# Low parts of a drain moved between VectorE and GpSimd, and the down-projections' waits moved to where each weight piece is used

## The chip, the cores and the metric

The kernel runs on one core of a Trainium2 chip. The time is device microseconds of one launch. The kernel before takes 1396.87 us (median of 3 runs, 1396.63 to 1397.98).

## The reference, cut to what matters

Two layers of a diffusion transformer over 256 tokens `x` and 256 context tokens `ctx`, width 1024. Layer zero mixes with a gated linear attention (hgrn2, 8 heads, forward and backward), layer one with a Mamba-2 mixer; each is followed by a convolutional feed-forward block of width 2816.

```python
for l in range(DEPTH):                                  # 2
    mx = split(silu(c) @ ada_w[l] + ada_b[l], 6)        # shifts, scales and gates
    hx = modulate(rmsnorm(x, pre_norm[l, 0]), mx[0], mx[1])
    yx = mixer(hx, hc)                                  # l = 0: hgrn2, l = 1: mamba2
    x = x + mx[2] * rmsnorm(yx, post_norm[l, 0])
    hx = modulate(rmsnorm(x, pre_norm[l, 1]), mx[3], mx[4])
    x = x + mx[5] * rmsnorm((silu(conv(hx @ w_up_a)) * (hx @ w_up_v)) @ w_down, post_norm[l, 1])
# hgrn2, per head and direction: f = lb + (1 - lb) * sigmoid(fz); k = 1 - f
# att = tril((q * exp(cumsum log f)) @ (k * exp(-cumsum log f)).T), plus the state carried between chunks
# y = (rmsnorm(o) * norm_w * silu(g)) @ hg_w_out
```

In layer zero the same is done for `ctx`, so its stages have 512 columns (`T`), those of layer one after the mixer 256 (`SEQ`).

## The kernel before, in words

All products of weights run as three matmuls of split numbers: a tile's high part times a weight's high part, its low part times the high part, and its high part times the weight's low part (`gemm`, L2095 to L2097). A weight arrives in pieces of 128 x 1024 (`subs`, 4 slots of `wraw`). For each piece SP loads it (`load`, L609), ScalarE writes the high part `wh` (`split_hi`, L799), VectorE or GpSimd writes the low part `wl` = `wraw` - `wh` (`split_lo`, L1312; `part`, L700), and TensorE waits for the count of low parts (`need_sub`). Activations are split likewise: ScalarE writes `hh` (`y_high`, L984), and the low part `hl` = `yT` - `hh` is written by VectorE's `y_low` (L1562) or GpSimd's (L745).

Each engine's order is written out by hand; semaphores are counted. Stage one is the hgrn2 mixer: for each of 8 heads, VectorE's `gate_products(h, d)` works in two halves, forward (d = 0) and backward (d = 1). A half clamps ScalarE's exponential (L1591, `e_clamped`), lets ScalarE take logarithm, exponential and logarithm again (L940 to L944), scans (L1607 or L1609), lets ScalarE take three exponentials (L949 to L953, `en_ready`), and forms the products (L1644 to L1657), with `qk_ready` after L1656 and `qin_ready` after L1657.

The drain is the end of this stage, the last head (7), whose own attention has no next head's projections to lie beside. TensorE's order there is: `att(7, 0)`, `ke(7, 0)`, the first k-tiles of the output projection's tiles 0 to 2 (`hg_early((0, 1), range(3))`, L2299 to L2301; it needs pieces 40 to 42 and the low parts 0 and 1 of `yT`), `kv(7, 0)` (L2237; it waits for ScalarE's `ke_rows`, L978), an ada block (L2161), `o_turn(6)` (L2268), `att(7, 1)` (L2210), `ke(7, 1)` (L2228; its bank must be emptied by `states(7, 0)`, L1536 and L1540), and then further k-tiles. Pieces 40 to 47 are the eight column tiles of the output projection.

GpSimd does nothing between the constants and this drain; then it waits for all of `qin_ready` and writes the low parts 2 to 6. VectorE writes 0, 1 and 7. `split_lo(42)` stands in `gate_products(7, 0)` between the small sums (L1633) and the wait on `en_ready`; `split_lo(43)`, `mask_att(7, 0)` and `states(7, 0)` stand after `gate_products(7, 1)`.

Each feed-forward block works in two halves of 12 and 10 k-tiles. A column tile of the down-projection takes two pieces, the first with 8 k-tiles, the second with the other 4 or 2, and TensorE waits for both before the tile's first matmul. Inside a tile, `need(k)` waits for GpSimd's low parts of the activations (`fl_ready`, L720) at the first and the last k-tiles. In the first half the eight tiles run in a loop, in the second they are written out. VectorE splits the pieces of the first down tile between the taps of the last convolution tile, and the next two behind it.

## Time and profile before

| | |
|---|---|
| median of 3 runs | 1396.87 us |
| the profiled execution | 1396.92 us |
| its span | 1395.2 us |
| TensorE (PE) busy | 1327.7 us, 95% of the span |
| VectorE (DVE) busy | 901.8 us, 65% |
| ScalarE (ACT) busy | 646.6 us, 46% |
| GpSimd (POOL) busy | 304.5 us, 22% |

The busy share is an average over stages with different limits; what a change is worth is read from the stage in which it lies. Times of a row are us from the start of the span. PE is a matmul, PEld a weight load that overlaps it, SPq the queue of the engine that issues DMAs.

### The profile page before, as it was taken

The page shows a single profiled execution, that of the slowest core. Times are in us where ns is not written, and L with a number is a line of the kernel's source. Part 1 is how long each engine was busy: PE and PEld are TensorE (multiplying, and loading weights), DVE is VectorE, ACT ScalarE, POOL GpSimd, SP SyncE. Part 2 cuts the span into 40 slices and gives each one's busy share as a digit, 9 for nine tenths or more (in the row PEclk, how much of TensorE's full clock was granted, in tenths as well). Part 3 has the DMA queues.
Part 4 walks back from the last instruction along what each step waited for, and adds up shares of the span by engine and source line. Part 5 has one row for each costly group of instructions (what it writes and reads, how often), then busy time and mean ns, then how long its engine had stood idle before and what let it go on. Part 6 is the DMA issues. An engine that isn't in the chain of part 4 may idle for free.

```text
span 1395.2 us, 21261 instructions
## 1 busy us (share of the span) xinstructions
PE 1327.7 (95%) x7893; PEld 1116.3 (80%) x7893; DVE 901.8 (65%) x1730; ACT 646.6 (46%) x1020; POOL 304.5 (22%) x203
## 2 busy tenths in 40 slices
PE   5999999999998999999999989999999988899997
PEld 3678888888665788888888757888888877899997
DVE  5567777677588644322456778777777957765573
ACT  4435444444355533223333256555555645554554
POOL 1000000000200654105551000211111300680961
PEclk9999999999999999999999999999999999999999
DMA  9543343335461632334324424433333465455743
GB/s 346 178 133 124 121 132 126 122 96 177 151 210 32 181 94 72 90 105 121 91 68 136 121 91 121 151 91 91 92 93 98 128 216 147 120 167 170 207 136 107
DMA packets 274787, 183.16 MB, mean 131 GB/s; under 512 B 6642, under 2 KB 249106, under 8 KB 274706
## 3 DMA queue, kind: packets, MB, share of 16 engines
q1 hardware_dynamic: 274162, 180.00, 42.7%
q10 hardware_dynamic: 544, 2.10, 0.4%
q8 instruction: 49, 0.80, 0.2%
q14 instruction: 32, 0.26, 0.1%
HBM read 181.03 MB, written 1.05 MB: 131 GB/s over the span
## 4 chain that ended last, share of the span: by engine, by line
PE 77%; DVE 12%; ACT 6%; issue 2%; DMA 1%; SPq 1%; POOL 0%; DVEq 0%; ACTq 0%
PE bank L2095 20%; PE bank L2097 20%; PE bank L2096 20%; DVE wl L1312 2%; PE bank L2161 2%; ACT tmp L845 1%; DMA gates<-in_ada_w 1%; ACT wh L799 1%; DVE hl L1408 1%; DVE tmp L1430 1%; PE bank L2210 1%; DVE conv L1760 1%; PE bank L2237 1%; PE bank L2665 1%; ACT hh L849 1%
## 5 line engine op out<-in xcount | busy, mean ns | idle before, releaser
L2095 PE MATMUL bank<-hh,wh 128*128 128x512 f32 (+1 forms) x1298 | 460.2, 355 | 11.1 <-DVE wl L1312 5.5
L2097 PE MATMUL bank<-hh,wl 128*128 128x512 f32 (+1 forms) x1298 | 455.5, 351 | 0.0
L2096 PE MATMUL bank<-hl,wh 128*128 128x512 f32 (+1 forms) x1298 | 455.2, 351 | 0.0
L799 ACT ACTIVATE wh<-wraw 128x1024 fp32r<-128x1024 f32 (+2 forms) x265 | 256.4, 985 | 99.6 <-PE bank L2097 97.3
L1312 DVE TENSOR_TENSOR wl<-wraw,wh 128x1024 fp32r<-128x1024 f32 (+2 forms) x187 | 206.0, 1124 | 121.7 <-ACT wh L799 121.6
L2095 PEld LDWEIGHTS bank<-hh,wh 128*128 128x128 f32 x1298 | 246.8, 190 | 45.9 <-DVE wl L1312 7.8
L2097 PEld LDWEIGHTS bank<-hh,wl 128*128 128x128 f32 x1298 | 246.7, 190 | 32.4
L2096 PEld LDWEIGHTS bank<-hl,wh 128*128 128x128 f32 x1298 | 247.0, 190 | 30.3
L1760 DVE SCALAR_TENSOR_TENSOR conv<-bank,pv,conv 128x189 f32<-128x189 f32 (+3 forms) x396 | 173.3, 438 | 131.7 <-ACT conv L1064 103.6
L700 POOL TENSOR_TENSOR wl<-wraw,wh 128x1024 fp32r<-128x1024 f32 x78 | 186.9, 2406 | 316.6 <-ACT wh L799 316.0
L2095 PE MATMUL bank<-fh,wh 128*128 128x512 f32 (+1 forms) x352 | 120.0, 341 | 3.5 <-DVE wl L1312 3.1
L2096 PE MATMUL bank<-fl,wh 128*128 128x512 f32 (+1 forms) x352 | 119.0, 338 | 0.0
L2097 PE MATMUL bank<-fh,wl 128*128 128x512 f32 (+1 forms) x352 | 119.0, 338 | 0.0
L745 POOL TENSOR_TENSOR hl<-yT,hh 128x512 fp32r<-128x512 f32 x13 | 18.5, 1448 | 371.6 <-DVE gates L1657 357.9
L2095 PEld LDWEIGHTS bank<-fh,wh 128*128 128x128 f32 x352 | 66.2, 188 | 12.1 <-issue 1.7
L2097 PEld LDWEIGHTS bank<-fh,wl 128*128 128x128 f32 x352 | 66.2, 188 | 8.0
L2096 PEld LDWEIGHTS bank<-fl,wh 128*128 128x128 f32 x352 | 66.3, 188 | 7.9
L777 POOL TENSOR_TENSOR wx<-xtok,wtk 128x512 f32<-128x512 f32 x16 | 16.9, 1055 | 246.0 <-ACT xtok L1197 162.1
L2110 PE MATMUL bank<-hh,wh 128*128 128x512 f32 (+2 forms) x119 | 48.7, 409 | 15.2 <-DVE hl L1408 14.0
L1064 ACT ACTIVATE conv<-bank,pv 128x512 f32<-128x512 f32 (+1 forms) x44 | 29.4, 668 | 72.8 <-PE bank L2097 72.8
L720 POOL TENSOR_TENSOR fl<-prod,fh 128x512 f32 (+3 forms) x44 | 49.9, 1134 | 55.1 <-ACT fh L1080 55.1
L2110 PEld LDWEIGHTS bank<-hh,wh 128*128 128x128 f32 (+1 forms) x119 | 24.2, 203 | 30.3 <-issue 11.9
(337 smaller groups left out, 1918.9 us busy)
## 6 DMA issues: line engine op xcount, KB each, us to landing
wraw<-in_ffn_w_up SPq DMA_DIRECT2D x88, 512.0 KB, 3.9
araw<-in_ada_w SPq DMA_DIRECT2D x40, 1024.0 KB, 7.0
wraw<-in_mb_w_in SPq DMA_DIRECT2D x48, 512.0 KB, 4.0
wraw<-in_hg_w_in SPq DMA_DIRECT2D x40, 512.0 KB, 3.8
wraw<-in_ffn_w_down SPq DMA_DIRECT2D x32, 512.0 KB, 3.9
wraw<-in_mb_w_out SPq DMA_DIRECT2D x16, 512.0 KB, 4.6
gates<-in_ada_w SPq DMA_DIRECT2D x5, 1024.0 KB, 9.3
wraw<-in_hg_w_out SPq DMA_DIRECT2D x8, 512.0 KB, 4.8
```

Source lines behind the costliest of these rows:

```text
L700: pool.tensor_tensor(wl[:, n % SLOTS, 0:size], wraw[:, n % SLOTS, 0:size], wh[:, n % SLOTS, 0:size].bitcast(F32), ALU.subtract).then_inc(w ...
L720: pool.tensor_tensor(fl[:, bass.ds(i * 2 + c, 1), 0:w], prod[:, c % 2, 0:w].unsqueeze(1), fh[:, bass.ds(i * 2 + c, 1), 0:w].bitcast(F32), ...
L745: pool.tensor_tensor(hl[:, k, :], yT[:, k, :], hh[:, k, :].bitcast(F32), ALU.subtract).then_inc(yl_ready, 1)
L799: act.activation(wh[:, n % SLOTS, 0:size], wraw[:, n % SLOTS, 0:size], ACT.Copy).then_inc(w_hi, 1)
L1064: act.activation(conv[:, u, 0:n], bank[2 * u if src is None else src][:, 0:n], ACT.Identity, scale=pv[:, bass.ds(i * 2 + (cw + c), 1)], bi ...
L1312: ins = dve.tensor_tensor(wl[:, s, lo:hi], wraw[:, s, lo:hi], wh[:, s, lo:hi].bitcast(F32), ALU.subtract)
L1760: ins = V.scalar_tensor_tensor(out=o(conv[:, u, :]), in0=src(bank[up]), scalar=pv[:, bass.ds(i * 2 + (cw + row * FT + c), 1)], in1=o(conv[ ...
L2095: pe.matmul(dst, W, hi(k), start=(k == 0), stop=False, **skip)
L2096: pe.matmul(dst, W, lo(k), start=False, stop=False, **skip)
L2097: ins = pe.matmul(dst, L, hi(k), start=False, stop=(k == nk - 1), **skip)
L2110: pe.matmul(dst, W, hi(k), start=(k == 0), stop=False, skip_group_check=True)
L2161: ins = pe.matmul(bank[plan.bank(key)][32 * j:32 * j + 32, :], scc[:, 4 * half + j, :], ada_chunk(n, half, j), start=(half == 0), stop=(ha ...
```

## The change

In the drain, the low parts 0 and 1 of `yT` go from VectorE to GpSimd, ahead of GpSimd's wait on `qin_ready`; `mask_att(7, 0)` takes the place of `y_low(1)` inside `gate_products(7, 1)`; and `split_lo(42)` goes from before the wait on `en_ready` to behind the last product of `gate_products(7, 0)`. In the down-projections, TensorE waits for a tile's first piece before the tile and for the second at the k-tile that first uses it; the last tile of layer zero keeps both waits ahead of it.

```diff
@@ gpsimd
+        y_low(0, range(2))
         pool.wait_ge(qin_ready, 2 * HEADS)
         y_low(0, range(2, KT - 1))
@@ vector, gate_products(h, d)
             if end:
                 head_mean(HEADS - 2)
-                y_low(0)
             dve.wait_ge(sig_ready, n + 1)
...
             if h < HEADS - 1:
                 split_lo(5 * h + 6 + d)
-            elif d == 0:
-                split_lo(5 * h + 7)
-            else:
+            elif d == 1:
                 head_norm(HEADS - 2)
-                y_low(1)
+                mask_att(h, 0)
             dve.wait_ge(en_ready, n + 1)
...
             V.tensor_tensor(ch(Dd), ch(C), s[:, 1, :].unsqueeze(2).to_broadcast([P, NCH, CH]), ALU.mult).then_inc(qin_ready, 1)
+            if h == HEADS - 1 and d == 0:
+                split_lo(5 * h + 7)
@@ vector, after the heads
         split_lo(at["y", 0, 3])
-        mask_att(HEADS - 1, 0)
         states(HEADS - 1, 0)
@@ tensor, down-projection, first half
                         for u in range(2):
-                            for j in range(2):
-                                by, count = lo_of[d0 + 2 * u + j]
-                                pe.wait_ge(w_lo[by], i * 4 + count)
+                            by, count = lo_of[d0 + 2 * u]
+                            pe.wait_ge(w_lo[by], i * 4 + count)
                             pe.wait_ge(plan.freed["act"], i * 2 + (reads["act"] + u - 1))
-                            gemm(bank[4 + u][:, 0:n], tile_w(d0 + 2 * u), fhi, flo, nf, need=need).then_inc(psum_ready, 1)
+
+                            def need_both(k, u=u):
+                                if k == KT:
+                                    by, count = lo_of[d0 + 2 * u + 1]
+                                    pe.wait_ge(w_lo[by], i * 4 + count)
+                                need(k)
+
+                            gemm(bank[4 + u][:, 0:n], tile_w(d0 + 2 * u), fhi, flo, nf, need=need_both).then_inc(psum_ready, 1)
@@ tensor, down-projection, second half
                         need_sub(d0 + 2 * m)
-                        need_sub(d0 + 2 * m + 1)
...
                         if l == 0 and m == KT - 1:
+                            need_sub(d0 + 2 * m + 1)
                             last_tile(1, 0, 1, n, key, tile_w(d0 + 2 * m), fhi, flo, nf)
...
                         plan.wait_free(pe, key)
-                        plan.done(gemm(bank[plan.bank(key)][:, 0:n], tile_w(d0 + 2 * m), fhi, flo, nf, need=need), key)
+
+                        def need_last(k, m=m):
+                            if k == KT:
+                                need_sub(d0 + 2 * m + 1)
+                            need(k)
+
+                        plan.done(gemm(bank[plan.bank(key)][:, 0:n], tile_w(d0 + 2 * m), fhi, flo, nf, need=need_last), key)
```

## Rows read from the trace of the kernel before

**Rows 1.** Page, part 4: shares of the chain that ended last, by engine.
```profile
PE 77%; DVE 12%; ACT 6%; issue 2%; DMA 1%; SPq 1%; POOL 0%; DVEq 0%; ACTq 0%
```

**Rows 2.** TensorE's waits: line, releaser, us in total, times, longest.
```profile
PE bank L2299 <- DVE hl L1562: 2.4, 1, 2.4
```

**Rows 3.** Chain of waits, 340 to 430 us: start, us, what.
```profile
358.70 0.79 PE bank L2299
...
362.49 0.67 PE bank L2237 x6
...
365.01 0.59 PE bank L2268 x4
...
367.47 0.59 PE bank L2228 x4
```

**Rows 4.** Timeline of VectorE, drain: start, us, instructions, idle before and its releaser.
```profile
346.97 1.22 DVE L1312 TENSOR_TENSOR wl<-wraw,wh 128x1024 fp32r<-128x1024 f32 x1
348.10 0.68 DVE L1644 TENSOR_TENSOR gates<-tmp,gates 128x512 f32<-128x512 f32 x1
...
351.38 0.69 DVE L1657 TENSOR_TENSOR gates<-gates,sm 128x512 f32<-128x512 f32 x1
351.98 0.42 DVE L1591 TENSOR_SCALAR gates<-gates 128x512 f32<-128x512 f32 x1
...
353.76 0.55 DVE L1604 TENSOR_SCALAR gates<-gates,omlb 128x512 f32<-128x512 f32 x1 [0.17 <-ACT gates L942]
...
361.23 0.68 DVE L1656 TENSOR_TENSOR gates<-gates,sm 128x512 f32<-128x512 f32 x1
...
364.52 0.73 DVE L1540 SCALAR_TENSOR_TENSOR st<-st,sm,bank 128x128 f32<-128x128 f32 x2
```

**Rows 5.** Timeline of ScalarE, drain.
```profile
347.45 0.25 ACT L953 ACTIVATE sm<-sm 128x80 f32<-128x80 f32 x1
...
350.21 1.15 ACT L984 ACTIVATE hh<-yT 128x512 fp32r<-128x512 f32 x2
...
358.47 0.59 ACT L978 ACTIVATE ket<-bank 128x512 f32<-128x512 f32 x1
```

**Rows 6.** Instructions of line L745: duration in ns, least, median, most.
```profile
L745 POOL TENSOR_TENSOR hl<-yT,hh x13: 1262/1292/2193, 362.6 to 1127.4; 128x512 fp32r<-128x512 f32 x13
```

**Rows 7.** Timelines of VectorE and GpSimd, 1250 to 1290 us, where they meet.
```profile
1261.66 2.36 DVE L1312 TENSOR_TENSOR wl<-wraw,wh 128x1024 fp32r<-128x1024 f32 x2
1265.85 1.83 DVE L1312 TENSOR_TENSOR wl<-wraw,wh 128x1024 fp32r<-128x1024 f32 x2 [1.83 <-ACT wh L799]
...
1262.27 1.20 POOL L720 TENSOR_TENSOR fl<-prod,fh 128x256 fp32r<-128x256 f32 x1 [3.59 <-ACT fh L1080]
```

**Rows 8.** Timelines of GpSimd and VectorE, 1104 to 1108 us.
```profile
1104.48 8.71 POOL L745 TENSOR_TENSOR hl<-yT,hh 128x512 fp32r<-128x512 f32 x6
...
1106.22 1.51 DVE L2018 TENSOR_TENSOR h<-hs,bc 128x256 f32<-128x256 f32 x1
```

**Rows 9.** Stretches: us, busy PE, PEld, DVE, ACT, POOL (instructions), granted clock, DMA.
```profile
358.50:360.00 1.50, 1.30 (x3) 1.11 (x4) 1.47 (x4) 1.50 (x5) 0.00 (x0) 0.50 0.24 57
...
415.76:418.37 2.61, 0.00 (x0) 0.03 (x1) 2.61 (x7) 0.75 (x3) 0.00 (x0) 1.00 0.61 170
418.37:422.00 3.63, 3.63 (x9) 1.71 (x10) 2.58 (x5) 2.15 (x4) 0.00 (x0) 1.00 0.43 129
```

**Rows 10.** Timelines of TensorE and VectorE: start of `hg_early`, entries of layer one's down-projections.
```profile
354.00 0.48 PE L2299 MATMUL bank<-hh,wh 128*128 128x512 f32 x1
...
1256.89 1.21 DVE L1312 TENSOR_TENSOR wl<-wraw,wh 128x1024 fp32r<-128x1024 f32 x1
...
1257.74 0.60 PE L2173 MATMUL bank<-ident,asum 128*128 128x128 f32 x4
1259.86 0.36 PE L2095 MATMUL bank<-fh,wh 128*128 128x256 f32 x1 [1.52 <-DVE wl L1312]
...
1263.84 0.28 PE L2095 MATMUL bank<-fh,wh 128*128 128x256 f32 x1
...
1353.47 0.36 PE L2095 MATMUL bank<-fh,wh 128*128 128x256 f32 x1 [1.55 <-DVE wl L1312]
...
1357.28 0.39 PE L2095 MATMUL bank<-fh,wh 128*128 128x256 f32 x1 [0.38 <-POOL fl L720]
```

## The prediction

> **What bounds the kernel now.** I read the shares of the chain that ended last first: TensorE holds 77% of it, VectorE 12%, ScalarE 6% [rows 1]. So the time changes only where TensorE stands still, or where another engine carries the chain. TensorE's list of waits gives the places that the diff can touch. The plainest is one wait of 2.4 us for VectorE's `hl` of L1562 (`y_low`) [rows 2]. The chain of waits places it in the drain of stage one: at 358.70, and from there on TensorE's own work follows without a break [rows 3]. VectorE's timeline shows what stands ahead of it: `split_lo(42)` at 346.97, products up to L1657 at 351.38, the clamp L1591 of the next half at 351.98, then that half's products up to L1656 at 361.23 [rows 4]. Behind the wait the granted clock was 0.50 [rows 9].
>
> **The drain, VectorE's side.** (1) `split_lo(42)` leaves its place before the wait on `en_ready`. The product behind it, L1644, started at 348.10, but ScalarE's L953, for which it waits, ends at 347.45 + 0.25 = 347.70 [rows 4, 5]. L1644 can start at 347.74, so 0.36 us is gained; the rest of the 1.22 filled a wait. `qk_ready` of the first half comes 0.36 earlier, L1657 would start at 351.02 and make room at 351.62 (351.98 - 0.36).
> (2) The split now stands there, ahead of the clamp L1591, and takes 1.14 (348.10 - 346.97 by rows 4). ScalarE's three steps of the second half wait for that clamp, and VectorE's products for them. Clamp: 351.62 + 1.14 = 352.76 instead of 351.98, +0.78. Alone, the move makes the second half later. SP gains a late step too: the load that takes piece 42's slot waits for the split. Its own piece is used after 390 us, and what SP queues behind it waits for TensorE's next ada block anyway, so that costs nothing.
> (3) `y_low(0)` leaves VectorE in front of L1604, where VectorE waited for ScalarE with 0.17 us to spare [rows 4]: worth nothing. `y_low(1)` (0.60 to the next start) becomes `mask_att(7,0)` (0.63): +0.03. After the last product `states(7,0)` comes behind `split_lo(43)` alone, 0.63 sooner in the order.
> (4) The two low parts on GpSimd. ScalarE's two copies start at 350.21 and take 1.15 together [rows 5], the first is done by about 350.84, so GpSimd asks from 350.9, amid VectorE's L1656, L1657 and the moved split. A free L745 takes 1.26 to 1.29 us, the longest took 2.19 [rows 6]. What the engines do to each other shows where they met. At 1261.66 VectorE's two splits took 2.36, the same pair 1.83 at 1265.85, and GpSimd's `fl` took 1.20. Taken whole and in turns: first split to 1262.73, `fl` 0.74 to 1263.47, second split 0.55 to 1264.02, which is what the rows say to 0.01 [rows 7]. From 1104.48 six L745 took 8.71 us, and a VectorE product of 256 columns (L2018) took 1.51, twice what L1644 needs for 512 [rows 4, 8]. So a GpSimd instruction and a VectorE one with two inputs in SBUF exclude each other, and turns alternate even when the next of VectorE's is queued.
> By that: `y_low(0)` gets its turn at 351.03 and ends at 352.3; L1657 ends at 352.9; `y_low(1)` runs to 354.1; the moved split to 355.2; the clamp starts at 355.1, +3.1 us. If GpSimd gets no turn between L1656 and L1657, the clamp is at +2.1 (no further turn taken ahead of the clamp) to +3.3. The low end of (2) and (4) together is +0.8, with no hindrance at all. I take +3.1, by the nearest rows, two queued splits.
>
> The Trainium skill says more than the rows do (SBUF — State Buffer, section "SBUF: two separate sides"): GpSimd and VectorE share a pair of ports under an exclusive lock held for the whole instruction, against every VectorE instruction with two SBUF inputs. By that L1657 is hit as the splits are; were only splits hit, the clamp would come some 0.7 us sooner and the sum be that much smaller. The rule speaks against this half of the change, and rows 7 agree.
>
> **The drain, TensorE's side.** `att(7,0)` starts 0.36 earlier, so `hg_early` is reached at 353.65, before 354.00 [rows 10]. It needs pieces 40 to 42, and 42 is done at 355.2: TensorE idles 1.6 us in place of 2.37. Its 18 matmuls of 0.23 end at 359.5 (before: 362.49). Next late is `kv(7,0)`, which waits for ScalarE's L978; that stands behind the second half's exponents and ended at 358.47 + 0.59 = 359.06 [rows 5], 3.1 later is 362.2: a new idle of 2.7 us. `kv`, the ada block and the turn take 365.60 - 362.49 = 3.11 [rows 3], so `att(7,1)` starts at 365.3; its own `qk_ready`, 361.91 + 3.1 = 365.0, is just inside [rows 4]. `ke(7,1)` is 1.88 behind, at 367.2. But it wants the bank that `states(7,0)` empties: VectorE's products end at 365.6, the split of 43 takes 1.1, `states` 1.05: 367.8, against 367.47 before, +0.3 us. If the clock falls in the idle of 2.7 us, as it did in that of 2.37 (0.50 from 358.50 to 360.00), the 3.11 us of work lose about 1.4, and `ke(7,1)` starts at 368.6, +1.1. A gap of 2.61 us at 415.76 kept 1.00, so it need not fall [rows 9]. I take +1.1. GpSimd's `y_low(2)` ends at 368.0, in time; (3) to (6), 1.45 each by rows 8, end at 374, before TensorE asks. From there TensorE is without a wait to the end of the stage, and what follows hangs on it, so the shift stays.
>
> **The down-projections.** At the two entries of layer one TensorE stood still for a short second piece, 1.52 us to 1259.86 and 1.55 to 1353.47 [rows 10]. First: the first piece is split at 1256.89 + 1.21 = 1258.10, the ada turn ends at 1258.34, so the tile starts 1.5 us sooner. Its last k-step, though, also waits (`fl_ready`) for GpSimd's last `fl`, 1262.27 + 1.20 = 1263.47 [rows 7]. The k-steps are 0.356 apart, so the twelfth stood at 1263.84 and is wanted at 1262.3; it will start at 1263.52, and a restart costs 0.11. The second tile stood 0.06 for its own short piece, which is now waited for later. 0.3 us is left of 1.52. Second: there the tenth k-step already waited for `fl`, until 1357.28 [rows 10], and VectorE's, ScalarE's and GpSimd's way to it is untouched. Nothing is left of 1.55. TensorE's waits show none of this kind in layer zero: nothing. The moved wait stands once in each tile at a k-step between matmuls; three k-steps of each tile carry a wait for `fl` now, and where it is met long before the starts stay 0.12 apart. I take 0; bounds -0.1 and +0.3 us over all tiles. Behind it only the same tile's rest is queued.
>
> **Sum.** +1.1 - 0.3 = +0.8 us. The profiled execution took 1396.92 us (span 1395.2 and 1.7 around it), 0.05 over the median of the runs. Forecast: 1397.7 us. A measurement of this kernel tells about 0.2%, 2.8 us, from no change; the forecast is no change.
>
> **Rivals.**
> A. The engines don't hold each other up here. For it: L745 and the gate products have not met in this trace. Against: rows 7 and 8. The clamp is then 0.78 late only; TensorE runs to 357.9, waits for ScalarE to 359.9, `att(7,1)` is at 363.0, `ke(7,1)` at 365.5 by `states`, 1.95 earlier. With the 0.3 of the down-projections: 1394.7 us. 20%.
> B. The slower one: TensorE's clock at the next gap. At 415.76 it stood 2.61 us and kept 1.00, where the shorter one of 2.37 lost it [rows 2, 9]. So whether a gap of this length costs the clock depends on where it falls, and any shift of the drain moves it. Behind it stand the matmuls of the sums, 3.63 us busy on the chain [rows 9]; half speed through most of them costs about 1.9. It decides as soon as that stretch reads 0.50: 1397.7 + 1.9 = 1399.6 us. 22%.
> C. VectorE keeps its turn through the queued products, clamp at +2.1: `kv` at 361.2 after 1.7 us of idle with the clock kept, `ke(7,1)` at 366.8, -0.7. With the 0.3: 1395.9 us. 15%.
> D. The down-projections gain their full 3.07 us. For it: both idles are put down to `wl`. Against: `fl` is 0.4 us behind in the first and already waited for in the second. 1394.9 us. 3%.
>
> **How the numbers follow.** Forecast 40%, A 20, B 22, C 15, D 3. A and D lie 2 us below the median and pass 0.2% in about half of their cases, the clock at later gaps adding or taking up to 1.7: faster 0.15. B lies 2.7 above and passes it in half, and a tail of the forecast with it: slower 0.16. Same 0.69. The range reaches from just under A to just over B: 1394.3 to 1399.9.
>
> **What would show it.** Right: L745 twice near 351; L1657 or the moved L1312 longer than 0.69 and 1.22; the clamp near 355; TensorE's wait on L1562 gone, and in its place one of L2299 on L1312 and one of L2237 on L978; the first down tile of layer one from 1258 with an idle before its last k-step for L720. Wrong: a clamp before 353.5 (A), `ke(7,1)` before 366 us, a clock of 1.00 from `kv(7,0)` on, or an entry in layer one that gains over 1 us.

## The result, and the profile after

| | before | after |
|---|---|---|
| median of the runs (22 each) | 1396.92 us (1393.06 to 1398.86) | 1400.01 us (1397.21 to 1401.32) |
| the profiled execution | 1396.92 us, span 1395.2 | 1398.98 us, span 1397.2 |
| TensorE busy | 1327.7 us | 1327.1 us |
| VectorE busy | 901.8 us | 903.3 us |
| GpSimd busy | 304.5 us | 308.4 us |

The ratio after to before is 1.0016 [1.001, 1.0022]: 2.2 us slower (1.4 to 3.1), where 0.8 was forecast. It lies inside what was called no change, though the upper end of the interval passes the 2.8 us that were named for that, and its sign is certain. The medians of the table lie further apart, 3.1 us, because the times of the kernel after form two groups and the median falls into the upper one (the means lie 2.4 apart); the text goes by the ratio. By the ratio the kernel takes 1399.1 us, inside the range of 1394.3 to 1399.9; its median alone stands 0.1 us above it.

In the kernel after, line numbers are shifted by one or two: the split is L1313, the clamp L1592, the last two products L1654 and L1655, ScalarE's `ket` L979, `hg_early` L2298, `kv` L2236, `ke` L2227.

First comes VectorE's timeline in the drain of the kernel after (start, us, instructions, idle before and its releaser). It answers to [rows 4].

```profile
346.57 0.69 DVE L1642 TENSOR_TENSOR gates<-tmp,gates 128x512 f32<-128x512 f32 x1 [0.69 <-ACT sm L954]
...
349.25 0.68 DVE L1654 TENSOR_TENSOR gates<-gates,sm 128x512 f32<-128x512 f32 x1
349.85 1.76 DVE L1655 TENSOR_TENSOR gates<-gates,sm 128x512 f32<-128x512 f32 x1
351.54 2.28 DVE L1313 TENSOR_TENSOR wl<-wraw,wh 128x1024 fp32r<-128x1024 f32 x1
353.74 0.41 DVE L1592 TENSOR_SCALAR gates<-gates 128x512 f32<-128x512 f32 x1
355.52 0.55 DVE L1604 TENSOR_SCALAR gates<-gates,omlb 128x512 f32<-128x512 f32 x1 [0.77 <-ACT gates L943]
...
365.65 0.73 DVE L1541 SCALAR_TENSOR_TENSOR st<-st,sm,bank 128x128 f32<-128x128 f32 x2
```

Then GpSimd and ScalarE there, which answer to [rows 5, 6].

```profile
349.76 2.98 POOL L745 TENSOR_TENSOR hl<-yT,hh 128x512 fp32r<-128x512 f32 x2 [345.07 <-ACT hh L985]
```

```profile
346.29 0.25 ACT L954 ACTIVATE sm<-sm 128x80 f32<-128x80 f32 x1
...
360.24 0.58 ACT L979 ACTIVATE ket<-bank 128x512 f32<-128x512 f32 x1
```

The reader is to see the two engines take turns. GpSimd's two low parts run from 349.76 to 352.74. In that time the product L1655 takes 1.76 us instead of 0.69, and the moved split L1313 2.28 instead of 1.22: each is 1.07 and 1.06 us longer, the time for which it waited on one of GpSimd's low parts. The clamp behind them comes at 353.74.

TensorE's timeline in the drain of the kernel after, which answers to [rows 3], and then its granted clock by stretches, which answers to [rows 9] (us, busy PE, PEld, DVE, ACT, POOL, clock, DMA).

```profile
353.88 0.50 PE L2298 MATMUL bank<-hh,wh 128*128 128x512 f32 x1 [1.16 <-DVE wl L1313]
...
360.88 1.65 PE L2236 MATMUL bank<-vtok,ket 128*128 128x128 f32 x6 [2.62 <-ACT ket L979]
362.45 2.68 PE L2160 MATMUL bank<-araw,scc 128*32 128x512 f32 x16
...
367.53 0.66 PE L2227 MATMUL bank<-ident,gates 128*128 128x128 f32 x4
```

```profile
360.88:362.40 1.52, 1.52 (x6) 1.35 (x6) 1.49 (x5) 1.52 (x4) 0.00 (x0) 0.50 0.00 0
362.40:365.60 3.20, 3.20 (x22) 1.05 (x22) 3.20 (x7) 0.88 (x2) 1.24 (x1) 0.74 0.07 7
416.00:418.53 2.53, 0.00 (x0) 0.03 (x1) 2.53 (x6) 0.67 (x3) 0.00 (x0) 1.00 0.61 181
418.53:422.16 3.63, 3.63 (x5) 1.55 (x6) 2.57 (x5) 0.58 (x1) 0.00 (x0) 0.53 0.45 133
```

The sums and the entry of layer zero's up-projections, TensorE's timelines: first the kernel before, then the kernel after.

```profile
418.37 1.10 PE L2405 MATMUL bank<-sq,ones 128*128 128x512 f32 x2 [2.61 <-DVE sq L1381]
...
430.45 0.77 PE L2110 MATMUL bank<-hh,wh 128*128 128x512 f32 x1 [3.98 <-DVE hl L1408]
```

```profile
418.53 1.93 PE L2404 MATMUL bank<-sq,ones 128*128 128x512 f32 x2 [2.60 <-DVE sq L1382]
...
432.31 0.76 PE L2109 MATMUL bank<-hh,wh 128*128 128x512 f32 x1 [3.98 <-DVE hl L1409]
```

The wait for `hl` of L1562 [rows 2] is gone, and two stand in its place: 1.16 us for piece 42 and 2.62 us for `ket`. Behind the second the clock is 0.50. And behind the idle ahead of the sums at 418.53, 2.60 us long where it had been 2.61, the clock is 0.53 where it had been 1.00. From the first sum to the up-projections it is 13.78 us instead of 12.08.

The entries of layer one's down-projections, from TensorE's timeline of the kernel after; they answer to [rows 10].

```profile
1260.20 0.60 PE L2172 MATMUL bank<-ident,asum 128*128 128x128 f32 x4
...
1265.97 0.39 PE L2094 MATMUL bank<-fh,wh 128*128 128x256 f32 x1 [1.02 <-POOL fl L720]
...
1354.25 0.39 PE L2094 MATMUL bank<-fh,wh 128*128 128x256 f32 x1 [0.26 <-DVE wl L1313]
...
1359.34 0.39 PE L2094 MATMUL bank<-fh,wh 128*128 128x256 f32 x1 [1.63 <-POOL fl L720]
```

From the ada turn to the last k-step of the first tile it is 5.77 us instead of 6.10: 0.33 gained. Laid side by side, the two profiled executions give the whole account (start of the same instruction, us):

| | before | after | difference | what came since the line above |
|---|---|---|---|---|
| ScalarE's small exponential, forward half ("the mark") | 347.45 | 346.29 | -1.16 | +0.38 up to 89 us, then -1.54 by the clock behind an idle of 2.4 us there: 0.50 before, 1.00 after |
| `ke(7,1)` | 367.40 | 367.53 | +0.13 | the drain: +1.29 |
| first sum behind the output projection | 418.37 | 418.53 | +0.16 | |
| first up-projection, layer zero | 430.45 | 432.31 | +1.86 | the clock at the sums: +1.70 |
| first up-projection, layer one | 1178.76 | 1181.23 | +2.47 | the clock behind an idle of 2.93 us near 1129, 0.50 in both but for longer after: +0.61 |
| last k-step, first down tile | 1263.84 | 1265.97 | +2.13 | the down-projections: -0.33 |
| tenth k-step, ninth down tile | 1357.28 | 1359.34 | +2.06 | -0.07 |
| end of the span | 1395.2 | 1397.2 | +2.0 | |

The terms ahead of the mark and the one near 1129 lie where the change touches nothing. So one pair of executions does not price the change: its own terms are +1.29 in the drain, -0.4 in the down-projections, and perhaps the +1.70. The experiments had to settle whether the last belongs to it.

### The profile page after: what moved, and what is told of

It reads as the page before. It is cut to its first block, busy times and chain, and to the rows that moved or that the text cites. A ratio compares the mean times of both kernels' runs of the same rounds, so it can differ in the third digit from the quotient of the medians.

```text
span 1397.2 us, 21265 instructions
## 1 busy us (share of the span) xinstructions
PE 1327.1 (95%) x7893; PEld 1116.0 (80%) x7893; DVE 903.3 (65%) x1728; ACT 646.6 (46%) x1020; POOL 308.4 (22%) x205
## 4 chain that ended last, share of the span: by engine, by line
PE 77%; DVE 13%; ACT 7%; issue 2%; DMA 1%; POOL 0%; DVEq 0%; ACTq 0%
PE bank L2094 20%; PE bank L2096 20%; PE bank L2095 20%; DVE wl L1313 3%; PE bank L2160 2%; ACT tmp L846 1%; ACT wh L800 1%; DVE conv L1759 1%; DVE hl L1409 1%; DVE tmp L1431 1%; PE bank L2209 1%; PE bank L2236 1%; PE bank L2676 1%; ACT hh L850 1%; PE bank L2663 1%
## 5 line engine op out<-in xcount | busy, mean ns | idle before, releaser
L1313 DVE TENSOR_TENSOR wl<-wraw,wh 128x1024 fp32r<-128x1024 f32 (+2 forms) x187 | 207.0, 1129 | 121.6 <-ACT wh L800 121.5
L745 POOL TENSOR_TENSOR hl<-yT,hh 128x512 fp32r<-128x512 f32 x15 | 22.4, 1520 | 369.0 <-ACT hh L985 357.4
L720 POOL TENSOR_TENSOR fl<-prod,fh 128x512 f32 (+3 forms) x44 | 50.2, 1141 | 55.0 <-ACT fh L1081 55.0
```

Of the source, the lines that this page charges most:

```text
L720: pool.tensor_tensor(fl[:, bass.ds(i * 2 + c, 1), 0:w], prod[:, c % 2, 0:w].unsqueeze(1), fh[:, bass.ds(i * 2 + c, 1), 0:w].bitcast(F32), ...
L745: pool.tensor_tensor(hl[:, k, :], yT[:, k, :], hh[:, k, :].bitcast(F32), ALU.subtract).then_inc(yl_ready, 1)
L1313: ins = dve.tensor_tensor(wl[:, s, lo:hi], wraw[:, s, lo:hi], wh[:, s, lo:hi].bitcast(F32), ALU.subtract)
```

## The experiments

Positions are given in us behind the mark (the start of ScalarE's small exponential of the forward half), so that what happened earlier drops out. Before: clamp 4.53, `ket` 11.02, `kv(7,0)` 14.88, `ke(7,1)` 19.95 by the timeline (the chain of waits [rows 3] has this start 0.07 later). After: clamp 7.45, `ket` 13.95, `kv(7,0)` 14.59, `ke(7,1)` 21.24. Ratios are to runs of the kernel before on the same chip.

**One part alone.**

`down_only`: the kernel before with the down-projections' waits moved. Part of the edit is shown; the second wait goes to the k-tile that first uses the piece, as in the change.

```diff
-                            for j in range(2):
-                                by, count = lo_of[d0 + 2 * u + j]
-                                pe.wait_ge(w_lo[by], i * 4 + count)
+                            by, count = lo_of[d0 + 2 * u]
+                            pe.wait_ge(w_lo[by], i * 4 + count)
...
-                        need_sub(d0 + 2 * m + 1)
...
```

> Only the waits of the down-projections are changed, the drain is the one of before. My theory (the wait for fl takes the place of the wait for the short piece): the first down tile of layer one, first half, starts about 1.5 us sooner after the last up tile, then TensorE idles about 1.0 us before its last k-step for GpSimd's L720, and the eight tiles end 0.2 to 0.4 us sooner than before; second half: tile starts 1.2 us sooner and waits 1.6 us for L720 instead of 0.4, nothing is gained. Sum -0.3 us. Rival D (both idles are real gains): -3.1 us. Rival (waits inside a tile cost issue time): slower by 0.3 us or more. Times of single runs spread by some us from one to the next, so the verdict is read from the two entries.

Measured 1396.15 us (10 runs) against 1397.20, ratio 0.9997 [0.9987, 1.0006]. TensorE's timeline of this kernel at the same k-step:

```profile
1257.25 0.60 PE L2173 MATMUL bank<-ident,asum 128*128 128x128 f32 x4
...
1263.03 0.39 PE L2095 MATMUL bank<-fh,wh 128*128 128x256 f32 x1 [1.03 <-POOL fl L720]
```

5.78 us instead of 6.10, and the second entry's wait for `fl` grew from 0.38 to 1.64. The 1.52 and 1.55 us that stood on `wl` were worth 0.3 and less than 0.1, as the theory had it.

`split_only`: the kernel before with `split_lo(42)` behind the last product.

```diff
-            elif d == 0:
-                split_lo(5 * h + 7)
...
+            if h == HEADS - 1 and d == 0:
+                split_lo(5 * h + 7)
```

> Only split_lo(42) is moved behind the last product of the first half; both low parts stay on VectorE. Measured in the trace from the start of ScalarE's small exponential of the first half (L953, 347.45 before) to ke(7,1) (L2228, 367.47 before): 20.02 us before. My theory (the split filled a wait and now stands ahead of the clamp): clamp 4.53 + 0.78 = 5.3 us after that mark, and ke(7,1) at 20.8 us, +0.8. Rival (the split's 1.1 us come off the chain as a move to a place where it does not matter): 18.9 to 20.0 us.

Measured 1398.42 us (10 runs) against 1397.20, ratio 1.0005 [0.9995, 1.0014]. The clamp is at 5.31, 0.78 later than before, to the hundredth what steps (1) and (2) said. The split took 1.22 there: without GpSimd beside it, it is not long. `ke(7,1)` is at 20.21, +0.26 where +0.8 was expected, but the two profiles differ in the clock: this one kept 1.00 in the drain behind an idle of 2.69 us, the kernel before lost it behind 2.37. Against `before_clk` below, which keeps the clock too and has `ke(7,1)` at 19.43, it is +0.78, the full delay of the clamp.

`pool_only`: the kernel before with the two low parts on GpSimd; split and mask stay.

```diff
+        y_low(0, range(2))
         pool.wait_ge(qin_ready, 2 * HEADS)
...
-                y_low(0)
...
-                y_low(1)
```

> Only the two low parts go to GpSimd; split_lo(42) and mask_att(7,0) stay where they were. Mark as in split_only (20.02 us before to ke(7,1); clamp at 4.53 us). My theory (whole instructions in turns): GpSimd's first low part gets its turn behind L1656, L1657 takes 1.9 us in place of 0.69, and the clamp comes at 5.8 us if a tensor_scalar with one input is not hit, at 7.1 us if it is. ke(7,1) then at 18.6 us (bound by states) or at 19.8 to 20.6. Rival A (no hindrance): clamp at 4.5, L1657 0.69 us, ke(7,1) at 17.5 to 18.2.

Measured 1401.01 us (8 runs) against 1397.20, ratio 1.0024 [1.0014, 1.0035]. VectorE's timeline of this kernel, then TensorE's:

```profile
351.27 1.76 DVE L1656 TENSOR_TENSOR gates<-gates,sm 128x512 f32<-128x512 f32 x1
352.95 1.49 DVE L1592 TENSOR_SCALAR gates<-gates 128x512 f32<-128x512 f32 x1
```

```profile
361.16 0.94 PE L2236 MATMUL bank<-vtok,ket 128*128 128x128 f32 x6 [2.89 <-ACT ket L979]
...
366.07 0.86 PE L2267 MATMUL bank<-ident,tmp 128*128 128x128 f32 x4 [2.12 <-DVE attm L1552]
366.73 1.91 PE L2209 MATMUL bank<-gates 128*128 128x128 f32 x8
```

This is the dearest of the three parts. With no split queued, GpSimd's second turn falls on the clamp itself: 1.49 us instead of 0.42. It has only one input in SBUF, so the prediction had counted it as free of this, while the expectation of this run had left it open. And `o_turn(6)` waits 2.12 us for `mask_att(7,0)`, which still stands behind the second half's products. `ke(7,1)` is at 22.66, +2.71 and 2 us later than the latest that was expected. What lies beyond the expectation is mostly the clock: it was kept behind the idle of 2.89 us and lost behind the 2.12 us of this second wait (0.50 from 366.73 to 369.70; the eight matmuls of L2209 take 1.91 us instead of 1.06). From `o_turn(6)` to `ke(7,1)` it is 3.94 us, where `after_nomask` and `before_clk`, with the clock at 1.00 there, take 2.43 and 2.44: some 1.5 of the 2.71 us are the clock's.

`after_nomask` asks what the moved mask is worth: the kernel after with `mask_att(7,0)` put back behind `split_lo(43)`.

```diff
-                mask_att(h, 0)
...
+        mask_att(HEADS - 1, 0)
         states(HEADS - 1, 0)
```

> The changed kernel, but mask_att(7,0) stays behind split_lo(43) as before. Seen in pool_only: o_turn(6), which takes the bank that mask_att empties, waited 2.1 us for it. Theory (that move carries part of the change): o_turn waits about 2 us, ke(7,1) at 23 us or later after the mark in place of 21.2. Rival (mask_att's place is free either way): 21.2 us.

Measured, in one run, 1400.90 us. `o_turn(6)` waits 0.48 us for the mask and `ke(7,1)` is at 21.93: 0.69 later than in the kernel after, less than the theory had, because the lost clock ahead of it already makes `o_turn` late, and behind it no clock is lost as it was in `pool_only`. So the mask's new place takes back part of what the low parts cost.

**GpSimd kept off VectorE's queue.**

`gated`: the low parts go to GpSimd, but only once the last product of the forward half of head 7 is done; the split stays in its old place; mask and down-projections as in the change. GpSimd's part of the edit, against the kernel before:

```diff
+        pool.wait_ge(qin_ready, 2 * HEADS - 1)
+        y_low(0, range(2))
         pool.wait_ge(qin_ready, 2 * HEADS)
```

> The change, but split_lo(42) stays where it was and GpSimd waits for the last product of the first half (15 counts of qin_ready) before low parts 0 and 1, so that these lie beside VectorE's clamp, sum and waits for ScalarE. My theory: L1657 keeps 0.69 us, the clamp stays at 4.5 us after the mark, L1604 or the scan is delayed by 0 to 0.6 us by the second low part, TensorE runs hg_early without a wait and then idles about 1.4 us for ScalarE's L978 with its clock kept; ke(7,1) at 17.8 us after the mark (bound by states) in place of 20.0. With the down-projections' 0.3: 2.5 us faster than before, ratio 0.9982, more or less 1 us by TensorE's clock at later gaps. Rival (the low parts hold VectorE up wherever they lie): ke(7,1) at 20 us or later, time unchanged or slower.

Measured 1395.59 us (11 runs) against 1397.20, ratio 0.9988 [0.9979, 0.9998]. VectorE's timeline of this kernel, then GpSimd's:

```profile
350.54 0.68 DVE L1658 TENSOR_TENSOR gates<-gates,sm 128x512 f32<-128x512 f32 x1
351.15 0.42 DVE L1593 TENSOR_SCALAR gates<-gates 128x512 f32<-128x512 f32 x1
...
352.92 1.30 DVE L1605 TENSOR_SCALAR gates<-gates,omlb 128x512 f32<-128x512 f32 x1 [0.76 <-ACT gates L944]
```

```profile
351.31 2.63 POOL L745 TENSOR_TENSOR hl<-yT,hh 128x512 fp32r<-128x512 f32 x2 [346.62 <-DVE gates L1658]
```

The product takes 0.68 again and the clamp stands at 4.53, as before. The low parts now lie where VectorE waits for ScalarE's logarithm, and only L1605, again an instruction with one input, loses 0.75. Not every instruction with one input is hit: the `tensor_reduce` behind the clamp lies wholly beside GpSimd's first low part and takes 0.68 us, as it does in the kernel before with GpSimd idle. `ke(7,1)` is at 17.59: 2.36 us earlier than before and 3.65 earlier than after. The time is 1.7 us below that of the kernel before, where 2.5 was expected; this profile kept the clock in the drain and lost it at the sums. Against the kernel after, two things differ: what GpSimd's first instruction waits for, and the place of the split, which by `split_only` is worth 0.78 with the clock kept. No run moves the mask alone, so how much of the gain is GpSimd's stays open; an estimate for the mask is the 0.82 us that `o_turn(6)` waits for it in `before_clk`.

**The clock taken out.** These kernels put unused matmuls of 512 columns into TensorE's two idle times of 2.4 to 2.6 us, in the drain and ahead of the sums. They write a bank that is free and is overwritten afterwards.

`before_clk`: 8 ahead of the second k-tile of `hg_early`, 9 ahead of the sums, in the kernel before.

```diff
-        hg_early((0, 1), range(3))
+        hg_early((0,), range(3))
+        plan.wait_free(pe, ("kv", p, 0))
+        for _ in range(8):
+            pe.matmul(bank[plan.bank(("kv", p, 0))][:, 0:T], hh[:, 0, 0:P], hh[:, 0, :], start=True, stop=True)
+        hg_early((1,), range(3))
...
             plan.done(gemm(bank[plan.bank(key)][:, 0:n], w, hi, lo, nk), key)
+            if i == 0:
+                plan.wait_free(pe, ("am", LATE + 3))
+                for _ in range(9):
+                    pe.matmul(bank[6][:, 0:n], hh[:, 0, 0:P], hh[:, 0, 0:n], start=True, stop=True)
             both_sums(i, l, s, n)
```

> The kernel before, with matmuls added whose result is not used: 8 of 512 columns in the idle of 2.37 us in the drain (between the first and second k-tile of hg_early) and 9 in the idle of 2.61 us ahead of the sums (L2405). They only keep TensorE busy. Mark as before (start of the small exponential of the first half). My theory (the clock is a matter of where an idle falls in each execution, and the profile of before had lost it in the drain): granted clock 1.00 at both places in every profile, ke(7,1) at 18.4 us after the mark in place of 20.0, and the median 1 to 2 us below before, since both idles lose the clock in about half of the executions. Rival (the clock is not the matter, the waits alone set the time): ke(7,1) at 20.0 and the time unchanged or up to 0.5 us slower.

Measured 1395.97 us (11 runs) against 1396.98, ratio 0.9989 [0.998, 0.9998]. The clock is kept and `kv(7,0)` comes 1.39 sooner, at 13.49, but `ke(7,1)` only 0.52 sooner, at 19.43. TensorE's timeline of this kernel says why the expected 18.4 was missed:

```profile
361.20 0.83 PE L2237 MATMUL bank<-vtok,ket 128*128 128x128 f32 x6
...
364.70 0.63 PE L2268 MATMUL bank<-ident,tmp 128*128 128x128 f32 x4 [0.82 <-DVE attm L1551]
```

`o_turn(6)` takes over as the late one: it needs the bank that `mask_att(7,0)` empties. So of the clock lost in the drain of the kernel before, only half a microsecond was a cost.

`after_clk`: the same in the kernel after, with 9 between `hg_early` and `kv(7,0)`, and 9 ahead of the sums (the edit shows the first).

```diff
         hg_early((0, 1), range(3))
+        plan.wait_free(pe, ("kv", p, 0))
+        for _ in range(9):
+            pe.matmul(bank[plan.bank(("kv", p, 0))][:, 0:T], hh[:, 0, 0:P], hh[:, 0, :], start=True, stop=True)
         kv(p, 0)
```

> The changed kernel with matmuls whose result is not used: 9 between hg_early((0, 1)) and kv(7,0), in the idle of 2.62 us, and 9 ahead of the sums. My theory: clock 1.00 at both, ke(7,1) at 20.1 us after the mark in place of 21.2; against before_clk it is 1.7 us slower by the drain (20.1 - 18.4) less 0.3 of the down-projections, 1.4 us in all, and 1 to 2 us faster than the changed kernel. Rival (the extra loss over my forecast is a thing of the clock at the sums): after_clk is within 0.5 us of before_clk.

Measured 1396.69 us (11 runs) against 1396.98, ratio 0.9993 [0.9984, 1.0002]. TensorE's timeline of this kernel:

```profile
361.82 0.94 PE L2236 MATMUL bank<-vtok,ket 128*128 128x128 f32 x6 [0.59 <-ACT ket L979]
...
367.39 0.66 PE L2227 MATMUL bank<-ident,gates 128*128 128x128 f32 x4 [0.32 <-DVE st L1541]
```

`kv(7,0)` starts where it did, at 14.59, its six matmuls take 0.94 us instead of 1.65, and `ke(7,1)` is at 20.16, waiting for `states`. That is 1.08 less than in the kernel after. With the clock out of play at these two places on both sides, the change costs 0.9993 against 0.9989, +0.6 us, each ratio uncertain by 1.3 us; the drains differ by 20.16 - 19.43 = +0.73 and the down-projections by -0.4, which is +0.3. So the times don't part the theory (1.4 us slower than `before_clk`) from the rival (within 0.5), and the timelines speak for the rival. With the clock in play the change costs 2.2 (1.4 to 3.1). That the clock makes the difference between the two is the likely reading, but their intervals overlap.

`after_sums` and `after_drain` fill only one of the two idle times of the kernel after, the second and the first of the two edits above.

> The changed kernel with 9 unused matmuls of 512 columns ahead of the three sums behind the output projection, so that TensorE's idle there (2.60 us, clock 0.50 behind it) is mostly filled; the drain is left as it is (2.62 us idle, clock lost). Theory (the two new or longer idle times each cost the clock by themselves): behind the sums the clock reads 1.00 and the stretch to the next projection is about 1.7 us shorter than in the changed kernel; the drain keeps its local sum (ke(7,1) at 21.2 us behind the mark, or 20.2 if the clock happens to be kept there). Time: the changed kernel's ratio 1.0016 less 1.7 us, 1.0004. Rival (one clock loss brings on the other, because both idle times fall alike on whatever the chip looks at): with the sums filled nothing changes in the drain, and the gain is all of the 3 us that separate the changed kernel from the one with both filled, ratio 0.9993.

> The changed kernel with 9 unused matmuls between hg_early and kv(7,0), so that TensorE's new idle there shrinks from 2.62 to 0.59 us; the sums are left as they are. Theory: the drain as in the kernel with both filled, ke(7,1) at 20.2 us behind the mark (1.1 less than in the changed kernel), the clock at the sums (2.6 us idle) lost or kept by the execution. Time: 1.0016 less 1.1 us, 1.0008, down to 0.9993 if the sums keep their clock in most executions. Rival: the clock costs nothing in the drain, because VectorE's chain through states(7,0) sets ke(7,1) anyway: ke(7,1) at 21.2 and the ratio stays at 1.0016.

`after_sums`: 1395.64 us (11 runs) against 1397.08, ratio 0.9994 [0.9985, 1.0003]. The idle ahead of the sums is 0.53 us, the clock 1.00 behind it; in the drain the clock is still lost, from about 1.3 us behind the restart on instead of at once, and `ke(7,1)` is at 21.43. The time lies nearer to the rival's 0.9993 than to the theory's 1.0004, which is just outside the interval. Against the rival's mechanism, that one loss brings on the other, stand the profiles: `down_only` and the kernel before lost the clock in the drain alone, `split_only` and `gated` at the sums alone. Why the gain is 3.1 us and not 1.7 stays open.

`after_drain`: 1397.83 us (12 runs) against 1397.08, ratio 1.0003 [0.9995, 1.0012]. `ke(7,1)` is at 20.18, as with both filled, so the rival (VectorE sets `ke(7,1)` at 21.2 anyway) is out. TensorE's timeline of `after_drain`, in the drain and at the sums:

```profile
362.17 0.94 PE L2236 MATMUL bank<-vtok,ket 128*128 128x128 f32 x6 [0.60 <-ACT ket L979]
...
367.75 0.66 PE L2227 MATMUL bank<-ident,gates 128*128 128x128 f32 x4 [0.33 <-DVE st L1541]
...
418.72 1.10 PE L2407 MATMUL bank<-sq,ones 128*128 128x512 f32 x2 [2.59 <-DVE sq L1382]
...
430.81 0.77 PE L2109 MATMUL bank<-hh,wh 128*128 128x512 f32 x1 [3.98 <-DVE hl L1409]
```

Here the sums began at 418.72 behind an idle of 2.59 us with the clock at 1.00, and reached the up-projections 12.09 us later; in the kernel after it was 13.78 behind an idle of 2.60. Filling the sums alone clearly gains on 1.0016 [1.001, 1.0022]; for the drain alone the intervals still touch, and it is the timeline that shows its gain. The shares are not told apart well: the ratios give 3.1 and 1.8 us, the timelines 1.70 and 1.08, both fills together 3.2 and 2.78, and each ratio is uncertain by 1.3 us.

**A version that beats both, and where that ends.**

`gated_clk`: `gated` with the 9 unused matmuls ahead of the sums.

> The gated version (GpSimd waits for 15 counts of qin_ready, split_lo(42) in its old place, mask_att(7,0) and the down-projections' waits as changed) with the 9 matmuls of no use ahead of the sums. Theory: ke(7,1) at 17.6 us after the mark as in gated, the sums at full clock; 0.8 us below before_clk by the drain and 0.3 by the down-projections, 3 us below before: ratio 0.9978. Rival (gated's gain was a matter of the clock, not of the drain): no faster than before_clk.

Measured 1393.95 us (11 runs) against 1396.98, ratio 0.9975 [0.9966, 0.9984]: 3.5 us faster than the kernel before. `ke(7,1)` is at 17.58. Set against `before_clk`, which has the clock likewise out of play, it is 2.0 us faster, where the timelines give 1.85 in the drain and 0.4 in the down-projections.

`gated_more` adds unused 128-column matmuls at three entries where TensorE stands 4 to 5 us and the clock was 0.50 behind it. (Where its expectation says "the backward half", the kernel has the forward half, 15 counts of `qin_ready`.)

```diff
+                    for _ in range((9, 12)[l]):
+                        pe.matmul(bank[0][:, 0:P], ident[:, :], ident[:, :], start=True, stop=True)
                     by_tile(hl_count - KT, [up(0, 0), up(0, 1), up(1, 0), up(1, 1)], n)
...
+        for _ in range(16):
+            pe.matmul(bank[plan.bank(first[0])][:, 0:P], ident[:, :], ident[:, :], start=True, stop=True)
         by_tile(2 * KT, [(bank[plan.bank(key)][0:64, :]
```

> The best version so far (GpSimd's two low parts behind the last product of the backward half, the mask moved, the down-projections' waits, the sums' idle filled: 0.9975 of the kernel before) with unused 128-column matmuls also ahead of three entries where TensorE waits 4 to 5 us for VectorE's first low part: 9 ahead of layer zero's first up-projections (idle 3.98), 16 ahead of layer one's first projections (5.11), 12 ahead of layer one's up-projections (4.54). In each the granted clock read 0.50 for 3.3 to 5 us behind the restart. Theory (an idle time costs the clock behind it, and idle left of under 2 us doesn't): the clock reads 1.00 behind all three, each gives back half of its slow stretch, 1.7 + 1.6 + 2.4 = 5.7 us: about 1388 us, ratio 0.9934. Rival (VectorE sets the pace behind these entries, or the unused matmuls hold up the real ones): the clock reads 1.00 and the time stays within 1.5 us of 1394, 0.997.

Measured 1392.51 us (12 runs) against 1397.08, ratio 0.9976 [0.9967, 0.9984], against 0.9975 for `gated_clk`: no gain that can be told from noise, and far from the 0.9934 expected. TensorE's timeline of this kernel, then the clock of that stretch:

```profile
425.62 3.87 PE L2448 MATMUL bank<-ident 128*128 128x128 f32 x18 [2.60 <-DVE wl L1314]
```

```profile
425.62:429.24 3.62, 3.62 (x18) 3.62 (x19) 3.47 (x7) 1.34 (x3) 0.00 (x0) 0.53 0.54 148
```

The idle of 3.98 us, which the trace put down to `hl`, had been two waits in a row. TensorE first stood 2.60 us for the low part of a weight piece; the unused matmuls came behind that, at half clock, and themselves held up the real ones. The name at an idle time is that of the last wait.

`gated_fill` puts them ahead of the wait for the pieces. Part of the edit is shown; 16 more stand ahead of that wait at layer one's first projections.

```diff
                 if half == 0:
+                    for _ in range((11, 13)[l]):
+                        pe.matmul(bank[0][:, 0:P], ident[:, :], ident[:, :], start=True, stop=True)
                     need_sub(u0 + 2)
...
```

> As the version before it, but the unused 128-column matmuls (11, 16 and 13) stand ahead of TensorE's wait for the first weight pieces of the three entries, not behind it: in the version before, TensorE had first stood 2.60, 3.82 and 3.88 us for the low part of a piece, the clock was 0.50 when the unused matmuls began, and it stayed there. Theory (an idle time costs the clock behind it, so what counts is that no idle time before the restart is long): TensorE is busy for 2.5, 3.7 and 3.0 us of the 3.98, 5.11 and 4.54 us, the clock reads 1.00 behind all three in most executions, and 1.7 + 1.6 + 2.4 = 5.7 us come back: about 1388 us, ratio 0.9935. Rival (what VectorE and ScalarE deliver sets the pace behind these entries, the slow clock being hidden there): the clock reads 1.00 and the time stays at 1392.5 to 1394 us, 0.997.

Measured 1392.74 us (7 runs) against 1396.36, ratio 0.9976 [0.9964, 0.9987]: again no gain, though the edit now did what it was meant to. TensorE's timeline and clock of this kernel:

```profile
422.86 2.72 PE L2444 MATMUL bank<-ident 128*128 128x128 f32 x22
426.91 0.47 PE L2110 MATMUL bank<-hh,wh 128*128 128x512 f32 x1 [1.33 <-DVE hl L1410]
...
430.86 0.50 PE L2110 MATMUL bank<-hh,wh 128*128 128x512 f32 x1 [0.94 <-DVE hl L1410]
```

```profile
426.91:430.86 3.95, 3.00 (x13) 2.15 (x13) 3.58 (x8) 1.73 (x3) 0.00 (x0) 1.00 0.42 124
```

The clock is 1.00, and TensorE stands still again 3.95 us later, because VectorE delivers its low parts no faster. In `gated_clk` the same matmuls ran at 0.52, and the next low part of VectorE's was just in time. Laid side by side, VectorE's and ScalarE's instructions in the two profiles keep their distance within 0.1 us across each of the three entries, so none of them gave anything back. A slow clock behind an idle time costs only where TensorE is then the late one: at the sums and in the drain it is, at these three entries it is not. The rival was right.

## Why the prediction was right or wrong

**Steps (1) and (2), the split.** Right. It leaves 0.36 us and costs 1.14 in its new place; `split_only` has the clamp 0.78 later, as worked out.

**Step (3), low part and mask.** Right in the kernel after, where the exchange costs nothing, but it saw only half of it. `o_turn(6)` waits for the mask (2.12 us in `pool_only`, 0.82 in `before_clk`), and the prediction named no wait on `mask_att(7,0)`. The missed term is 0.69 us by `after_nomask`. It did no harm here, since the move takes that wait away in the kernel whose time was forecast; it is why `before_clk` gained less than was expected of it.

**Step (4), the two engines' turns.** Right in kind and size: L1655 took 1.76 and L1313 2.28 us, the clamp 7.45 behind the mark where the prediction says 355.1 - 347.45 = 7.65. Rival A (no hindrance, 1394.7) is out by these two rows, rival C (VectorE keeps its turn) by L1655. What is held up was bounded too narrowly, though. The prediction held only instructions with two inputs in SBUF to be hit; L1592 (1.49 instead of 0.42) and L1605 (1.30 instead of 0.55) have one. In the kernel after none of these meets GpSimd, so the sum did not suffer, but in `pool_only` it is the whole second turn. A `tensor_reduce` with one input was not held (0.68 us in `gated` and in the kernel before). The Trainium skill (SBUF — State Buffer, section "SBUF: two separate sides") has this: beside the instructions with two SBUF inputs it counts those in a mode that uses both of VectorE's ports. The trace agrees with it in that these two lines were held; it doesn't show in which mode they ran.

**TensorE's side.** Right: an idle of 1.16 us for piece 42 (1.6 said), one of 2.62 for `ket` (2.7), the clock at 0.50 behind it, `ke(7,1)` at 21.24 behind the mark (368.6 - 347.45 = 21.15). The drain cost +1.29 where +1.1 was said. `after_clk` (20.16) parts it into 1.08 for the clock and 0.21 for `states`, where 0.8 and 0.3 were said.

**The down-projections.** Right: 0.33 of 1.52 us, and 0.07 of 1.55, with the idle times turning up before the last k-steps for L720, as said. Rival D is out.

**The step that fell short** is the one that treated the clock at the next gap as one case or the other. Rival B had the mechanism and nearly the price: the clock lost behind the 2.6 us idle at the sums, 1.9 us said, 1.70 measured. But it was given 22% as something the changed kernel would either do or not do, and the forecast had none of it. The runs say that an idle time of this length is a chance in each execution: of the eight profiled kernels whose sums are not filled, five lost the clock there and three kept it, `after_drain` among them, which is the kernel after from the drain on. With the changed drain left as it is and only the sums filled, the ratio falls from 1.0016 to 0.9994, the full price or more. Forecast 0.8, plus 0.2 in the drain, less 0.1 in the down-projections, plus anything from none to all of 1.70, is 0.9 to 2.6 us; measured is 2.2 (1.4 to 3.1). So the mechanism of the forecast stood, and a term of 1.3 us (0.5 to 2.2) is missing, of the size of most of rival B's. That it is this term is likely and not shown: the kernel before may pay it in some of its executions too, no run fills the sums of the kernel before alone, and with both places filled the two kernels gain 1.5 and 3.2 us, each uncertain by 1.3. That the result came out as no change and inside the range owes something to the width of both: the range reached up to rival B for a reason that the forecast itself left out.

How often it is lost stays open. The 22 times of the kernel after form two groups, ten from 1397.21 to 1399.03 and twelve from 1399.99 to 1401.32, 2.1 us apart by their means. But the profiled execution, at 1398.98, is in the lower group and lost the clock at the sums; it kept it at 89 us, and was 1.5 us early by that. So several idle times take part in a group, and the groups give no rate for one. Why the changed kernel should lose it more often than the kernel before is also open. In the profiled executions the kernel before and `down_only` lost it in the drain and not at the sums, `split_only` and `gated` at the sums and not in the drain, and the kernel after, `after_nomask` and `pool_only` in both.

## What to carry to other kernels

Moving an operation from VectorE to GpSimd does not take it off VectorE's time where the two meet: here the VectorE instruction that met one of GpSimd's waited for its end, 0.75 to 1.07 us each time. Look at what stands in VectorE's queue when GpSimd's inputs become ready, and make GpSimd wait until VectorE itself waits; here a wait of that kind, with the split left where it was, turned +1.29 us in the drain into -2.36, of which half a microsecond is the clock that the kernel before lost there. An idle time of TensorE's that is named in the trace is worth only what the next wait behind it leaves, and its name is that of the last of several waits. Price the clock behind an idle time as a chance in each execution, and only where TensorE is the late engine afterwards.

## What the runs showed of the hardware

- VectorE's `tensor_scalar` with one SBUF input and an SBUF output, 512 fp32 columns wide, also waits for the end of a GpSimd instruction: 1.49 us instead of 0.42 (`pool_only`) and 1.30 instead of 0.55 (`gated`). A `tensor_reduce` with one SBUF input of the same width doesn't: 0.68 us beside GpSimd (`gated`) and without it (before).
- The same idle time loses TensorE's clock in one profile and keeps it in another. Behind that ahead of the sums (2.54 to 2.61 us) it kept 1.00 in the kernel before, `down_only` and `after_drain`, and fell to 0.50 in the kernel after, `split_only`, `pool_only`, `after_nomask` and `gated`. In the drain 2.37 (before), 2.40 (`down_only`), 2.62 (after) and 2.63 us (`after_sums`, `after_nomask`) lost it, 2.69 (`split_only`) and 2.89 (`pool_only`) kept it, and the 2.12 us that come next in `pool_only` lost it. So among these idle times the length does not decide. The 0.50 begins with the restart in some profiles and up to 1.3 us behind it in others (`after_sums`, in the drain).
- Unused matmuls that cut an idle time to 1.45 us or less kept the clock at 1.00 in each place where they stood ahead of the first wait; behind a first wait of 2.60 us they ran at 0.53 (`gated_more`).
